# Gated-recurrence heads: operands raised level by level with tables of gate products

## The reference, cut to what matters

```python
q = silu(q_raw) * 128 ** -0.5
f = sigmoid(f_raw)                    # the gate; lb is 0 here
k = sigmoid(-f_raw);  v = i_in
# chunk by chunk, G = cumsum(log f) inside a chunk
o_inter = (q * exp(G)) @ S
A[i, j]  = sum_k q[i, k] * exp(G[i, k] - G[j, k]) * k[j, k]     # j <= i
o        = o_inter + A @ v
S        = exp(G_last) * S + (k * exp(G_last - G)).T @ v
o = rmsnorm(o) * w * silu(g_raw)
```

## Time and profile before

| what | value |
|---|---|
| median of 3 runs | 1240.55 us (1239.95 to 1241.35) |
| span of the profiled execution, first to last instruction | 1238.1 us |
| PE busy | 1225.2 us, 99% |
| VectorE, ScalarE, GpSimd busy | 790.6, 706.3, 426.4 us |
| mean granted TensorE clock | 0.996 |

### The profile page before, as it was taken

One profiled execution on the slowest core, in us unless ns is written; L12 is line 12 of the kernel. 1 busy time (PEld: TensorE's weight loads), 2 busy tenths in 40 slices (PEclk: granted clock), 3 DMA queues, 4 the chain that ended last, 5 costly groups with the idle time before them and its releaser, 6 DMA issues.

```text
span 1238.1 us, 20337 instructions
## 1 busy us (share of the span) xinstructions
PE 1225.2 (99%) x7494; PEld 1005.2 (81%) x7494; DVE 790.6 (64%) x1671; ACT 706.3 (57%) x1373; POOL 426.4 (34%) x260
## 2 busy tenths in 40 slices
PE   9999999999999999999999999999999999999998
PEld 8777777778877777788776888888988889889897
DVE  6766677775476766585798545684672257375575
ACT  6666666675437777645667886753432254353442
POOL 0000000004310000054486884122255476676663
PEclk9999999999999999999999999999999999999999
DMA  5322243443333323253132022331363322313322
GB/s 206 110 68 86 86 157 125 127 137 112 101 95 102 103 86 99 80 179 124 39 100 71 18 84 69 105 136 37 118 207 117 119 85 71 135 69 137 102 69 68
DMA packets 38416, 128.17 MB, mean 104 GB/s; under 512 B 4640, under 2 KB 7584, under 8 KB 38320
## 3 DMA queue, kind: packets, MB, share of 16 engines
q1 hardware_dynamic: 35792, 121.91, 29.9%
q10 hardware_dynamic: 2528, 4.98, 1.3%
HBM read 123.43 MB, written 2.13 MB: 101 GB/s over the span
## 4 chain that ended last, share of the span: by engine, by line
PE 89%; issue 4%; DVE 2%; POOL 2%; ACT 2%; DMA 0%; ACTq 0%; DVEq 0%; POOLq 0%
PE G L1039 18%; PE G L1041 17%; PE G L1040 17%; PE S L1878 2%; PE S L1166 2%; PE O L1227 2%; PE G L2101 2%; PE G L2102 2%; PE G L2103 2%; PE T L1206 1%; PE S L1393 1%; PE T L1440 1%; PE O L1456 1%; PE S L1896 1%; POOL pieceL L682 1%
## 5 line engine op out<-in xcount | busy, mean ns | idle before, releaser
L620 POOL TENSOR_TENSOR wL<-w,wH 128x1024 fp32r<-128x1024 f32 x89 | 219.9, 2476 | 713.7 <-ACT wH L2256 713.7
L1039 PE MATMUL G<-hi,wH 128*128 128x512 f32 x1032 | 417.6, 405 | 0.4 <-DVE xT L1134 0.4
L1041 PE MATMUL G<-hi,wL 128*128 128x512 f32 x1032 | 404.0, 391 | 0.0
L1040 PE MATMUL G<-lo,wH 128*128 128x512 f32 x1032 | 403.6, 391 | 0.0
L1039 PEld LDWEIGHTS G<-hi,wH 128*128 128x128 f32 x1032 | 194.2, 188 | 48.6 <-issue 9.7
L1041 PEld LDWEIGHTS G<-hi,wL 128*128 128x128 f32 x1032 | 194.3, 188 | 42.4
L1040 PEld LDWEIGHTS G<-lo,wH 128*128 128x128 f32 x1032 | 194.6, 189 | 38.0 <-issue 1.2
L2256 ACT ACTIVATE wH<-w 128x1024 fp32r<-128x1024 f32 x140 | 147.6, 1056 | 107.3 <-DMA w<-weights_dram 53.3
L2833 DVE TENSOR_TENSOR wL<-w,wH 128x1024 fp32r<-128x1024 f32 x51 | 62.3, 1221 | 11.0 <-ACT wH L2256 10.2
L1156 DVE CUSTOM_DVE_ANT_0 adaw<-adaw,scr 128x1024 f32<-128x1024 f32 x31 | 52.3, 1686 | 0.2 <-issue 0.2
L1194 ACT ACTIVATE scr<-scr,sa 128x256 f32<-128x256 f32 (+2 forms) x64 | 35.2, 557 | 23.7 <-DVE sa L1181 23.7
(11 more groups left out here) (559 smaller groups left out, 2617.4 us busy)
## 6 DMA issues: line engine op xcount, KB each, us to landing
w<-weights_dram SPq DMA_DIRECT2D x150, 512.0 KB, 3.5
adaw<-ada_dram SPq DMA_DIRECT2D x43, 512.0 KB, 4.3
wp<-weights_dram SPq DMA_DIRECT2D x20, 512.0 KB, 4.5
kd<-c_dram ACTq DMA_DIRECT2D x8, 512.0 KB, 3.7
cbias<-ada_dram SPq DMA_DIRECT2D x5, 512.0 KB, 4.2
xT<-x_dram SPq DMA_DIRECT2D x4, 512.0 KB, 7.8
out_dram<-xT SPq DMA_DIRECT2D x8, 256.0 KB, 2.3
scr<-ca_dram SPq DMA_DIRECT2D x2, 512.0 KB, 5.0
```

Source lines behind the costliest of these rows:

```text
L620: g.tensor_tensor(wL[:, u.slot], raw_home(u), wH[:, u.slot].bitcast(f32), ALU.subtract).then_inc(w_lo, 1)
L1039: mm(home[:, :], whi, H[:, k, :], start=(k == first), stop=False)
L1040: mm(home[:, :], whi, L[:, k, :], start=False, stop=False)
L1041: last = mm(home[:, :], wlo, H[:, k, :], start=False, stop=(k == final))
```

## The change: what it does

It replaces the differences of log gates by products. One table per head is the gate itself, f = exp(log gate), in bank S[0] (`factor`, the only exponential left of `decay`); VectorE clamps it at 1e-30 (`clamped`) and forms from it, by seven reductions with multiplication, the products over 2, 4, 8, ... 128 neighbouring tokens (`powers`, into bank S[1] and `dec`). Then q and k stand in one pair of tiles and are raised in place: q by its own gate (`raise_q`), then at each level n, m = 2^(n-1), the second-half q by the product of the first-half gates and the first-half k by the product of the second-half gates (`raise_both`), 512 elements per level. Levels now go from small m to large, with products and raises in strict turns: product p reads what raise p-1 wrote, raise n overwrites what product n read.

TensorE loses `turn_g` and `diff` (with their constant matrices and their three DMAs); the values' product with the early half of each chunk is one matmul of 128 columns in place of two of 64 (`early_rows`), and comes before the wait for the state. `turn_ke`, `updates` and `states_of` of head t move from window t into window t+1. The 15 pairs of convolution terms are dealt as 4, 7, 4, 0 to the windows (before, 8 and 7 to the first two). ada blocks: none in the windows; 4 in the first block's output stage, 6 in the output stage that follows the heads, and these use the normal double buffer. Homes of output units 2 and 3 and of the late halves move from T to S.

```diff
-            def diff(t, j):
-                ...
-                for c in range(3 if j == KE else 4):
-                    last = mm(S[j % 2][:, c * P:(c + 1) * P], gT[:, c * P:(c + 1) * P], steps[j], start=True, stop=True)
-            def decay(t, e):
-                ...
-                s.activation(src[:, 0:w], src[:, 0:w], ACT.Exp).then_inc(sem("h_exp"), 1)
-                    v.tensor_tensor(pairs(here), pairs(raised[:, :]), kq_of(m), ALU.mult).then_inc(sem("h_x"), 1)
+            def factor(t):
+                act.wait_ge(sem("h_g"), t + 1 + since("h_g"))
+                if t:
+                    act.wait_ge(sem("h_aT"), 7 * t + since("h_aT"))
+                ...
+                s.activation(power(1), gl, ACT.Exp).then_inc(sem("h_exp"), 1)
+            def powers(t):
+                ...
+                for m in (1, 2, 4, 8, 16, 32, 64):
+                    link(v.tensor_reduce(dec[:, t % 2, :] if m == 64 else power(2 * m), power(m).rearrange("p (n a) -> p n a", a=2),
+                                         AX.X, ALU.mult))
+            def raise_both(t, n):
+                m = 1 << (n - 1)
+                dve.wait_ge(sem("h_products"), 8 * t + (2 if n == 1 else n + 1) + since("h_products"))
+                dve.wait_ge(sem("h_x"), 8 * t + n + since("h_x"))
+                by = power(m).rearrange("p (n a) -> p a n", a=2).unsqueeze(3).broadcast_to((P, 2, SEQ // (2 * m), m))
+                v.tensor_tensor(moved_on(t, m), moved_on(t, m), by, ALU.mult).then_inc(sem("h_x"), 1)
```

The start of TensorE's order in a window (`opened`; after it `fill` and `product` take turns), the last window's order, and ScalarE's order in a window:

```diff
+            def opened(t):
+                turn_ke(t - 1)
+                fill(t, 0)
+                updates(t - 1)
+                fill(t, 1)
+                outputs(t - 1)
+                product(t, 0)
+                product(t, 1)
+                fill(t, 2)
+                product(t, 2)
+                turn_h(t)
+                sum_h(t - 1)
+                fill(t, 3)
+                product(t, 3)
+            def last_window():
+                ...
+                product(3, 7)
+                output_m(2, (4, 5, 6))
+                turn_ke(3)
+                output_m(2, (7, 0))
+                output_m(0, (2,))
+                updates(3)
+                output_m(1, (2,))
+                output_m(2, (1,))
+                outputs(3)
+                output_m(2, (2,))
+                output_m(3, (4, 5))
+                sum_h(3)
+                output_m(3, (6, 7, 0, 1, 2))
...
             def window(t):
+                queries(t)
+                take_ke(t - 1)
+                ...
+                take_hv(t)
+                root_h(t - 1)
+                ...
+                if t == 2:
+                    act.wait_ge(sem("conv_sqsum"), 1)
+                    rsqrt_scalar(link, 1, 1.0 / 256, sem("conv_var"), sem("conv_root"))
+                if t < 3:
+                    keys(t + 1)
+                    factor(t + 1)
+                if t == 2:
+                    for k in range(2):
+                        act.wait_ge(sem("conv_z"), k + 1)
+                        silu_scalar_1(act, link, "cv", k, cacc[:, k, :], cv_th[k])
+                take_first(t)
```

VectorE's order in a window (`level_of` is `raise_both` and then `joined`). In the last window the high parts of the convolution's result are rounded by ScalarE behind `root_h`:

```diff
+            def window(t):
+                queries_1(t)
+                powers(t)
+                silu_vector_2(dve, "h", t - 1, zraw[:, :], zsig,
+                              mark("h_gated", t - 1) if t > 1 else (sem("a_gated_lo"), 10))
+                states_of(t - 1)
+                queries_2(t)
+                raise_q(t)
+                ...
+                raise_both(t, 1)
+                joined(t, 0)
+                joined(t, 1)
+                if t == 3:
+                    conv_gate()
+                    conv_low()
+                level_of(t, 2)
+                normed_h(t - 1)
+                gated_h(t - 1)
+                level_of(t, 3)
+                silu_vector_1(dve, "h", t, zraw[:, :], zsig)
+                low_h(t - 1)
+                level_of(t, 4)
+                if t == 2:
+                    conv_centre()
+                level_of(t, 5)
+                if t < 3:
+                    gates(t + 1)
+                level_of(t, 6)
+                if t < 3:
+                    clamped(t + 1)
+                raise_both(t, 7)
+                if t == 2:
+                    conv_scale()
```

More of the change, by code:

```diff
@@ L1991, in window, with first_window @@
-            def window(t):
-                if t:
-                    diff(t, KE)
-                fill(t, 0)
-                if t:
-                    diff(t, QE)
-                diff(t, LV0)
-                if t:
-                    outputs(t - 1)
+            def first_window():
+                product(0, 0)
+                product(0, 1)
+                gemm_h(1, 0, (0, 1))
+                product(0, 2)
+                turn_h(0)
+                gemm_h(1, 0, (2, 3, 4))
+                product(0, 3)
+                gemm_h(1, 0, (5, 6, 7))
+                product(0, 4)
+                gemm_h(1, 1, (0, 1))
+                product(0, 5)
+                gemm_h(1, 1, (2, 3))
+                product(0, 6)
+                gemm_h(1, 1, (4, 5))
+                product(0, 7)
+                gemm_h(1, 1, (6, 7))
@@ L2001, in window @@
                 if t == 2:
                     conv_sum()
-                fill(t, 1)
-                diff(t, LV0 + 1)
-                turn_ke(t)
-                product(t, 0)
-                product(t, 1)
-                product(t, 2)
+                fill(t, 5)
+                product(t, 5)
+                fill(t, 6)
+                product(t, 6)
                 if t == 2:
                     conv_sqsum()
-                fill(t, 2)
-                diff(t, LV0 + 2)
-                turn_h(t)
@@ L2078, in _ @@
             spread_c(pe, 1)
-            for t in range(4):
-                window(t)
-            output_m(0, (2,))
-            outputs(3)
-            output_m(1, (2,))
-            sum_h(3)
-            output_m(2, (4, 5, 6, 7, 0, 1, 2))
-            output_m(3, (4, 5, 6, 7))
-            for n in range(3):
+            first_window()
+            window(1)
+            window(2)
+            last_window()
+            for n in range(4):
                 output_m(n, (3,))
-            output_m(3, (0, 1, 2, 3))
             for n in range(4, 6):
@@ L3334, in _ @@
             gate_c(dve, 1)
-            operand(0, 1)
-            operand(0, 2)
-            for t in range(4):
+            first_window()
+            for t in range(1, 4):
                 window(t)
-            joined(3, 7)
             silu_vector_2(dve, "h", 3, zraw[:, :], zsig, mark("h_gated", 3))
-            blocks(9, 10)
+            states_of(3)
             normed_h(3)
```

566 lines of the change are left out of this document (213 added, 353 removed).

## The result

The kernel after takes 1257.43 us (median of 4 executions, 1256.59 to 1258.28), the kernel before 1240.25 (1239.35 to 1241.35). The ratio is 1.0142, with a 95% interval of 1.0129 to 1.0155: slower by 17.2 us, where 6.8 us faster was forecast. The profiled execution took 1258.17, its span is 1256.4 and its mean granted clock 0.986; before it was 0.996.

A forecast was written before the change was run, and what follows sets the result against it. The prediction took TensorE's own list as the bound: 35.7 us off it less 28.9 us of holes gave 6.8 us off the span, 1231.3, and 1233.8 us with the median's 2.45 us; range 1217 to 1243.

The forecast's parts named there:

- the last term of the sum: First block's output stage: four ada blocks moved there cost 0.3 us (0 to 3), the queue order being the same.
- two falls in the heads as they are: Clock in the heads: two falls stay as before, each costing 1.6 us; no further falls in the sum.
- the first term: TensorE's list: differences, gate transposes, merged outputs and the differences' waits come off, together 35.7 us.
- heads 1 and 2: Holes from waits for state, query, the norm's chain and a late turn_ke(2): 5.5 us (2 to 11).
- head 3, updates(2): Last window: updates waits for take_ke(2), behind convolution SiLUs and query steps on ScalarE; 6.3 us (4 to 9).
- product 3, product 4: Head 3: raise 2 behind conv_low, 2.6 us (0 to 4); norm before raise 3, 1.7 us (0 to 3).
- end norm, first (3,) tile: End of head 3: norm chain of 6.95 us covered by only five k tiles; hole 3.6 us (3 to 5).
- splits: Output unit 4 reuses unit 0's slot and waits for its rounding and subtraction; 1.5 us (0 to 2).
- output stage m: Output stage after the heads: six ada blocks on VectorE delay add_square 5, 2.0 us (0 to 5).
- the clock follows the holes: Rival: long holes bring three more clock falls, 5 us, giving 1238.6 us; chance 0.14.
- The raises are slow: Rival: raises on VectorE take 1.87 us instead of 0.69, 19 us more, giving 1253 us; chance 0.14.
- The holes close: Rival: VectorE and ScalarE run ahead, less than half of the holes stay (14 us), giving 1219 us; chance 0.22.

The follow-up runs named there:

- Experiment 2: Kernel before with only four ada blocks moved into the first block's output stage, in the change's load order; 1251.55 us, ratio 1.0100.
- experiments 1: Kernel after with the activations row and first two blocks of the first block's output stage loaded ahead of three weight units; 1251.56 us, ratio 1.0092.
- 6: Kernel after with those early loads, and the third and fourth block of the first output stage one residual later; 1247.59 us, ratio 1.0062.
- experiment 10: Kernel before with only the four blocks moved, their loads early and two of them one residual later; 1240.32 us, ratio 1.0010.
- experiment 11: Kernel after with all repairs together plus three further orders of work on ScalarE and VectorE, same arithmetic; 1227.63 us, ratio 0.9903.
- experiments 8: Kernel after with every repair together (early loads, later blocks, late gates, reordered convolution, head 3 and last output stage), same arithmetic; 1237.48 us, ratio 0.9983.
- Experiments 3: Kernel after with 24 useless matmuls in TensorE's wait of 6.26 us before updates(2) in the last window; 1262.51 us, ratio 1.0186.
- 4: Kernel after with the convolution's two SiLUs behind head 3's queries and the copy of head 2's turned keys ahead of them; 1252.75 us, ratio 1.0106.
- 7: Kernel after with VectorE's gates and clamp of the next head moved behind the seventh raise; 1257.49 us, ratio 1.0158.
- experiment 5: Kernel before with only the four blocks moved, plus 35 useless matmuls in TensorE's 8.30 us wait; 1250.85 us against 1251.55 without them.

## Why the prediction was wrong, point by point

**The step that failed** is the last term of the sum: "The four in the first block's stage: 0.3 (0 to 3, the same queue order)". It measured 12.2 us, 9.3 of idle time and 2.9 of clock. Experiment 2 shows it alone (11.7), experiments 1 and 6 take most of it back by SP's order and two moved positions, and in experiment 10 the same four blocks on VectorE cost nothing clear of noise. The term had one ground, that the queue's order stays the same. It does, but the order had never been early enough for a reader in this stage. Three things could be read before the change: SP's two loads at 302.20, VectorE at its third residual at 298.99, and the 6.0 and 6.9 us from issue to landing of just those two, where the page's median is 4.3. With 12.2 in place of the 0.3 the forecast would have been 1245.7, on the right side, but still 12 us short.

**A second step failed:** the clock, of which I left "two falls in the heads as they are" and put nothing more into the sum. The forecast span was 1231.3 and the measured one is 1256.4, 25.1 us apart. The four blocks are 11.9 of that, the clock elsewhere some 6.5, the size of the first term 3.6, and the other holes together 3.1.

**The other holes** were mostly foreseen, each by following the three lists:

| place | forecast | measured |
|---|---|---|
| before head 0 | 1.5 | 2.2 (0.83 + 0.91 + 0.42) |
| head 0 | 3.9 | 3.5 (0.45 + 3.07) |
| heads 1 and 2 | 5.5 | 8.0 (4.87 + 3.17) |
| head 3, updates(2) | 6.3 | 6.26 |
| product 3, product 4 | 2.6, 1.7 | 2.39, 1.61 |
| end norm, first (3,) tile | 3.6 | 3.59 |
| splits | 1.5 | 0.46 |
| output stage m | 2.0 | 3.6 |
| first block's output stage | 0.3 | 9.3 |

Not foreseen in heads 1 and 2 is product 7 of head 1, 2.74 us behind `gates(2)`: I had seen that in head 0 only. In the last output stage (m) the sixth block waited 1.77 us for its load behind the two buffers, and blocks took 1.4 to 2.7 us each. The holes come to 41, where 28.9 stood.

**What comes off TensorE's list**, 35.7: the records are right (7494 to 7198), the size a little too large. 34.4 of it was work (the rest were waits). In the kernel of experiment 11, where the clock is nearly what it was, TensorE is busy for 1225.2 - 1196.8 = 28.4 us less. Its clock is 0.994, not 0.996, which can hide 0.002 x 1200 = 2.4 us more: 30.8 us. This is worked out, not measured by itself. One reading in the prediction is a little low: 12 matmuls in 2.86 us are 0.72 a k tile, not 0.69; 0.69 leaves out what the change from small to large costs, which the prediction adds elsewhere.

**The clock.** The rival "the clock follows the holes" had a chance of 0.14 and a price of 5 us for three more falls. Of the two falls of before and then of the six of after, each stretch goes about from where the matmuls are slow to where they are back at speed. A PEclk of 0.50 is the lower of the two levels, 1.2 GHz, and 1.00 the upper, 2.4 GHz (busy us of each engine, PEclk, DMA share, GB/s):

```profile
808.80:812.10 3.30, 3.30 (x9) 2.60 (x8) 3.30 (x7) 1.71 (x3) 0.00 (x0) 0.50 0.36 119
842.50:846.50 4.00, 4.00 (x12) 2.66 (x12) 0.00 (x0) 0.60 (x1) 0.00 (x0) 0.57 0.00 0
```

```profile
310.40:315.66 5.26, 5.26 (x13) 4.11 (x13) 5.09 (x8) 3.33 (x5) 2.38 (x1) 0.50 0.00 0
715.33:718.70 3.37, 3.37 (x22) 2.76 (x22) 1.79 (x5) 1.33 (x3) 2.18 (x2) 0.51 0.51 156
810.16:814.20 4.04, 4.04 (x13) 3.46 (x14) 3.80 (x9) 1.58 (x2) 2.06 (x1) 0.50 0.00 0
831.44:835.00 3.56, 2.77 (x7) 1.66 (x5) 3.46 (x4) 0.33 (x1) 0.94 (x1) 0.55 0.42 130
865.05:869.00 3.95, 3.95 (x10) 3.15 (x11) 1.99 (x3) 2.46 (x4) 1.33 (x1) 0.57 0.00 0
892.11:899.50 7.39, 7.39 (x37) 7.39 (x38) 3.35 (x11) 2.74 (x7) 0.42 (x1) 0.54 0.02 9
```

Busy time times the clock that is missing gives 12.65 us for the six and 3.37 for the two, thus 9.3 us more. This is an estimate, since not all work in such a stretch need go at the clock's pace. Each of the six falls comes behind a wait of TensorE: 8.2, 3.1, 6.3, 2.4, 3.6 and 3.6 us. But a wait isn't the whole rule: behind the 2.74 us before product 7 of head 1 the clock stayed at 1.00, and the two falls of before have no wait at all ahead of them, only small products. Falls behind long holes should have had a price in the sum, not only in a rival. The Trainium skill ("TensorE: Matmul & The Clock Gate", HAM oscillation) says that an idle TensorE falls back to 1.2 GHz. Behind the holes of 8.2, 6.3, 3.6, 3.6, 3.1 and 2.4 us this trace agrees.

**The sum, redone:** 35.7 less 3.6 for its size, less 41 of holes, is 8.9 us slower. The span grew by 18.3, so 9.4 us are left for the clock. The six stretches give 9.3, and the same 7198 records keep TensorE busy for 1204.6 us in after and for 1196.8 in experiment 11, 7.8 us less.

**The rivals.** "The raises are slow" is wrong: L3147 in after is the answer to L3187 of the earlier trace rows,

```profile
L3147 DVE TENSOR_TENSOR kd<-kd,S 128x512 f32<-128x512 f32 x28 | 19.1, 683 | 17.9 <-PE S L1880 8.2 <-PE T L1880 7.2 <-PE T L1876 2.5
```

683 ns against 0.69 us. It was the only case that I let end slower, so that the right side had a chance of 0.14 for the wrong reason. "The holes close" did not happen by itself. It happened by hand, in experiments 8 and 11, and at another price: 1219 was given for 14 us of holes, and 1227.6 was reached with 15.6 us more idle time than before (28.5 against 12.9) and 30.8 instead of 35.7 us off the list.

## What to carry to other kernels

When work with a load of its own is moved to another stage, compare two times in the trace of before: when the load would be there (when its queue comes to it, by what waits ahead of it in that list, plus the landing time at that place), and when its reader will come. An engine's free time says nothing about that. And when a change shortens the list of the engine that is the bound, each hole costs its own length and often some of the clock behind it; before judging the change, reorder the lists of the others once, since the same arithmetic gave 1257 and 1228 us here.

## What the runs showed of the hardware that was not expected

**One late load cost more than its data.** The four blocks are 2 MB. Their loads landed 4.4 to 6.8 us after their issue, and the stage became 12.2 us longer, since SP's list reached the first load 3.1 us after its reader, and the third and fourth just as the reader came.

**Executions spread.** The kernel before lies within 2.0 us in the first comparison. Experiments 3, 4 and 7 spread by 6 to 7 us over four executions, with granted clocks that differ by 0.004 to 0.007 between executions of one kernel; experiment 11 spreads by 1.2. It isn't only a matter of holes: experiment 10 has hardly more idle time than before (14.9 against 12.9 us) and spreads by 4.4 us over ten executions, the kernel before by 3.7 over thirteen. The useless matmuls kept the clock up in one place (experiment 5) and only put its fall off in another (experiment 3). What decides between the two stays open.

**VectorE beside GpSimd.** A block of two SBUF operands took 1.22 us where GpSimd was idle. In the last output stage of the kernel of experiment 11 even an addition of 16 columns took 2.2 us; it ended within 0.1 us of GpSimd's pair of splits (timelines of GpSimd and then VectorE: start us, us):

```profile
855.49 5.70 POOL L613 TENSOR_TENSOR wL<-w,wH 128x1024 fp32r<-128x1024 f32 x2 [2.36 <-ACT wH L2253]
```

```profile
856.55 2.43 DVE L1165 CUSTOM_DVE_ANT_0 adaw<-adaw,scr 128x1024 f32<-128x1024 f32 x1
...
859.02 2.20 DVE L3296 TENSOR_TENSOR modT<-modsum,vecT 128x16 f32<-128x16 f32 x1
861.26 0.17 DVE L3297 SCALAR_TENSOR_TENSOR gainm<-modT,vecT 128x8 f32<-128x8 f32 x1
```

The next, as small, took 0.17, after the splits. The Trainium skill ("GPSIMD Engine Reference", Specifications) says that the interface is contended for operations with two SBUF inputs. These rows agree for the block and for the addition. I had taken 2.4 for each block of that stage, and the raises, with one SBUF operand, kept to 0.68.
